# RWKV chunk loop: one run of products without the inverse ahead of the levels, the rest in pieces between them

## The reference, cut to what matters

```python
def _rwkv7_step(state, inputs):
    r, decay, kk, a, k, v = inputs
    sa = jnp.einsum("bhvk,bhk->bhv", state, kk)
    state = (state * decay[:, :, None, :]
             - sa[..., None] * (kk * a)[:, :, None, :]
             + v[..., None] * k[:, :, None, :])
    y = jnp.einsum("bhvk,bhk->bhv", state, r)
    return state, y
```

## Time and profile before

| what | us |
|---|---|
| runs of the kernel before: median (lowest to highest of 3) | 4284.13 (4281.7 to 4284.21) |
| the profiled execution, span from the first to the last instruction (the one time shown for it) | 4290.0 |
| TensorE busy in it | 4142.7 |
| chunk loop in it, first score products to first matmul of the tail | 3017.1 to 3757.2 |

### The profile page before, as it was taken

One profiled execution on the slowest core, in us unless ns is written; L12 is line 12 of the kernel. 1 busy time (PEld: TensorE's weight loads), 2 busy tenths in 40 slices (PEclk: granted clock), 3 DMA queues, 4 the chain that ended last, 5 costly groups with the idle time before them and its releaser, 6 DMA issues. The chain is left out here.

```text
span 4290.0 us, 90861 instructions
## 1 busy us (share of the span) xinstructions
PE 4142.7 (97%) x35784; PEld 3330.7 (78%) x35784; DVE 2381.1 (56%) x3103; ACT 1664.3 (39%) x3296; POOL 816.2 (19%) x657
## 2 busy tenths in 40 slices
PE   7999999997999999999999999999899999999999
PEld 7888899886788888887666666666788888888887
DVE  5344454443444444444888877777566667633222
ACT  4222222223222222222666666666344444421112
POOL 3101111112111111101000000000356666600222
PEclk9999999998999999999999999999999999999999
DMA  2333333334333333335434443443333333365553
GB/s 90 116 120 120 111 110 106 106 100 144 97 106 114 100 107 114 116 117 153 87 82 88 89 92 85 86 85 71 96 98 101 101 101 101 86 204 174 189 184 125
DMA packets 482569, 479.81 MB, mean 112 GB/s; under 512 B 256784, under 2 KB 366992, under 8 KB 476128
## 3 DMA queue, kind: packets, MB, share of 16 engines
q1 hardware_dynamic: 469360, 445.85, 37.3%
q10 hardware_dynamic: 11520, 25.17, 1.6%
q0 software_dynamic: 1392, 4.54, 0.4%
HBM read 305.51 MB, written 169.93 MB: 111 GB/s over the span
## 5 line engine op out<-in xcount | busy, mean ns | idle before, releaser
L1271 DVE TENSOR_TENSOR_SCAN kept<-keep,kept 128x512 f32<-128x512 f32 (+1 forms) x448 | 436.6, 974 | 60.2 <-ACT keep L1233 18.7
L1233 ACT ACTIVATE keep<-z 128x512 f32<-128x512 f32 (+3 forms) x704 | 342.7, 505 | 230.5 <-PE z L1166 218.7
L1176 PE MATMUL turned<-t_identity,kept 128*128 128x128 f32 (+1 forms) x2432 | 376.0, 276 | 22.5 <-DVE kept L1271 22.5
L1243 ACT COPY w<-turned 128x512 f32<-128x512 f32 (+4 forms) x704 | 363.1, 528 | 79.7 <-PE turned L1176 78.2
L1176 PEld LDWEIGHTS turned<-t_identity,kept 128*128 128x128 f32 (+1 forms) x2432 | 277.7, 135 | 134.1 <-ACT w L1243 45.6
L1268 DVE TENSOR_TENSOR_SCAN kept<-keep,hidden 128x512 f32<-128x512 f32 (+3 forms) x256 | 284.2, 1116 | 133.7 <-ACT keep L1233 133.1
L1203 PE MATMUL acc<-w,dv 128*64 128x512 f32 (+3 forms) x1280 | 317.1, 554 | 0.0
L1165 PE MATMUL z<-k_high,q_parts 128*128 128x512 f32 (+3 forms) x704 | 300.0, 427 | 8.5 <-PEq L2210 5.3
L1165 PEld LDWEIGHTS z<-k_high,q_parts 128*128 128x128 f32 x704 | 133.4, 189 | 158.6 <-ACT keep L1233 96.8
L1166 PE MATMUL z<-k_low,q_parts 128*128 128x512 f32 (+3 forms) x704 | 250.6, 360 | 0.0
L1742 POOL TENSOR_TENSOR off<-NT,tri 128x512 f32<-128x512 f32 x165 | 206.0, 1275 | 167.6 <-ACT NT L1646 167.6
(11 more groups left out here) (566 smaller groups left out, 10814.7 us busy)
## 6 DMA issues: line engine op xcount, KB each, us to landing
w_raw0A<-in_w_main SPq DMA_DIRECT2D x42, 512.0 KB, 3.9
w_raw0B<-in_w_main SPq DMA_DIRECT2D x42, 512.0 KB, 4.0
w_raw1A<-in_w_main SPq DMA_DIRECT2D x41, 512.0 KB, 4.0
w_raw1B<-in_w_main SPq DMA_DIRECT2D x41, 512.0 KB, 3.8
KB<-scr_kb SPq DMA_DIRECT2D x33, 512.0 KB, 5.2
AR<-scr_ar SPq DMA_DIRECT2D x33, 512.0 KB, 5.2
y_raw<-scr_y SPq DMA_DIRECT2D x64, 256.0 KB, 4.5
merge<-scr_merge SPq DMA_DIRECT2D x64, 256.0 KB, 5.3
```

What stands on the lines that cost most here:

```text
L1176: mm = pe.transpose(turned[num % TB][0:size, P * r:P * r + P], kept[kept_in(g)][:, src:src + size], t["identity"][:, :])
L1233: act.activation(keep[num % KB][:, 0:size], z[num % ZB][:, 0:size], ACT.Sigmoid, scale=-DH ** -0.5).then_inc(keep_done, 1)
L1243: act.copy(w[num % WB][0:size, c0:512], turned[num % TB][0:size, c0:512]).then_inc(copied, 1)
L1271: dve.tensor_tensor_scan(dst, data, data, kept[kept_in(g)][:, end:end + 1], ALU.mult, ALU.bypass).then_inc(scanned, 1)
```

## The change

In turn `n`, TensorE now runs in one piece: the next state of chunk n-2, the score products of n, the variance of n-3, all value products of n-2, the key transposes of n itself, and half of the right sides of n-1. Then come the levels, with these pieces after the product and after the advance:

| level | after the product | after the advance |
|---|---|---|
| 1 | right sides of n-1, pairs 4 to 6 | pair 7 |
| 2 | own values; state outputs of n-1, pairs 0 to 2 | own values; pair 3 |
| 3 | own values; updates of n-1, pairs 0 to 2 | own values; pair 3 |
| 4 | updates, pairs 4 to 6 | pair 7 |
| 5 | state outputs, pairs 4 to 6 | pair 7 |

The next state of a chunk thus moves a turn later. `S_sum` and the state multiply are now first on their engines in a turn, `R` stands in level 2, `LV` in level 3, the `VU` copies in level 4. On ScalarE root, square, copy of `y_bank`, turned keys and `sq_high` come right behind the `NT` copies. The first half of the reciprocals is taken in four columns of 128x64, one in level 3, one in level 4, two in level 5; the other half stays 128x256 at the start of the next turn. `sq_low` stands behind the `off` masks. The diff, cut to its core (`heads` yields the pairs and heads that were two loops before):

```diff
@@ sync @@
                 if inside(n, -1):
-                    reach(sp, "st_pe", n - 1)
+                    reach(sp, "kbt_pe", n - 1)
                     load_keys(n + 1, nb)
...
                     if n == 2:
-                        reach(sp, "s_pe", n - 1)
+                        reach(sp, "r_pe", n - 1)
                     load_queries(n + 1, nb)
@@ tensor @@
+            def next_state(m):
+                b = m % 3
+                reach(pe, "u_even", m + 1)
+                reach(pe, "u_odd", m + 1)
...
+            def variance(m, n):
+                reach(pe, "sq_high", m)
+                reach(pe, "sq_low", m)
+                reach(pe, "kbt_out", 2 * min(n, NCH) - 1)
...
             def turn_keys(n):
                 b = n % 3
-                pe.wait_ge(kb_in[b], 16 * (n // 3) + 16)
                 reach(pe, "lv_out", n)
-                reach(pe, "std_done", n - 4)
+                reach(pe, "std_done", n - 3)
...
+            def right_sides(m, ks):
+                b = m % 3
+                reach(pe, "s_done", m)
...
+            def updates(m, ks):
+                b = m % 3
+                reach(pe, "r_out", m + 1)
+                reach(pe, "t_out", 10 * m + 10)
...
+            def state_outputs(m, ks):
+                b = m % 3
+                reach(pe, "yc_out", m - 1)
...
                 def beside_product(lv):
-                    if lv <= 2 and inside(n, 0):
-                        own_values(2 * lv - 2)
-                    if 3 <= lv <= 4 and inside(n, 2, 1):
-                        value_part(lv - 1)
-                    if lv == LAST and inside(n, -1):
-                        turn_keys(n + 1)
+                    if lv in (2, 3) and inside(n, 0):
+                        own_values(2 * lv - 4)
+                    if lv == 1 and inside(n, 1):
+                        right_sides(n - 1, (4, 5, 6))
+                    if lv == 2 and inside(n, 1, 1):
+                        state_outputs(n - 1, (0, 1, 2))
+                    if lv == 3 and inside(n, 1):
+                        updates(n - 1, (0, 1, 2))
+                    if lv == 4 and inside(n, 1):
+                        updates(n - 1, (4, 5, 6))
+                    if lv == 5 and inside(n, 1, 1):
+                        state_outputs(n - 1, (4, 5, 6))
...
-                if inside(n, 3, 1):
-                    variance()
-                if inside(n, 2, 1):
-                    value_part(0)
-                    value_part(1)
-                if inside(n, 1) and n < NCH:
-                    next_state()
+                if inside(n, 2) and n <= NCH:
+                    next_state(n - 2)
+                if inside(n, 0):
+                    score_products(n, turn)
+                if inside(n, 3, 1):
+                    variance(n - 3, n)
+                if inside(n, 2, 1):
+                    value_products(n - 2)
+                if inside(n, 0):
+                    turn_keys(n)
+                if inside(n, 1):
+                    right_sides(n - 1, (0, 1, 2, 3))
                 for lv in range(1, LAST + 1):
...
-            turn_keys(0)
             walk(pe, body)
@@ vector @@
-                if inside(n, 1):
-                    reach(dve, "r_pe", n)
-                    reach(dve, "lv_out", n)
-                    dve.tensor_tensor(R[:, :, :], chain[:, :, :], LV[:, :, :], ALU.add).then_inc(s["r_out"], 1)
+                if inside(n, 2) and n <= NCH:
+                    reach(dve, "s_pe", n - 1)
+                    reach(dve, "s_done", n - 2)
+                    dve.tensor_tensor(S_sum[:, :, :], chain[:, :, :], S[b2][:, :, :], ALU.add).then_inc(s["s_sum"], 1)
                 if inside(n, 4, 1):
-                    inverse_std(n - 4, 1)
+                    inverse_std(n - 4, slice(HP, PAIRS))
...
+                    if lv in (3, 4) and inside(n, 3, 1):
+                        inverse_std(n - 3, slice(lv - 3, lv - 2))
+                    if lv == LAST and inside(n, 3, 1):
+                        inverse_std(n - 3, slice(2, 3))
+                        inverse_std(n - 3, slice(3, 4))
...
-                if inside(n, 3, 1):
-                    inverse_std(n - 3, 0)
@@ gpsimd @@
-                if inside(n, 3, 1):
-                    reach(pool, "sq_high", n - 3)
-                    tt(sq_low[:, :, :], yc_sq[:, :, :], sq_high[:, :, :].bitcast(F32), ALU.subtract, "sq_low")
+                if inside(n, 2) and n <= NCH:
+                    reach(pool, "s_sum", n - 1)
+                    reach(pool, "ys_pe", n - 4)
+                    tt(S[(b + 2) % 3][:, :, :], S_sum[:, :, :], t["w_end"][:, bass.ds(n - 2, 1), :].rearrange(
+                        "p o k -> p (o k)").unsqueeze(2).broadcast_to(grid), ALU.mult, "s_done")
```

More of the change, by code:

```diff
@@ L1548, in own_values @@
+            def state_outputs(m, ks):
+                b = m % 3
+                reach(pe, "yc_out", m - 1)
+                for k, h, hs in heads(ks):
+                    mm = pe.matmul(y_bank[hs, k, :], S[b][hs, k, :], AR[b][hs, k, 1, :], start=k == 0, stop=False,
+                                   skip_group_check=True)
+                if ks[-1] == PAIRS - 1:
+                    mm.then_inc(s["ys_pe"], 1)
+            def body(n, b, turn):
                 def own_values(quarter):
@@ L1551, in own_values @@
                     reach(pe, "st_out", 2 * n + 2)
[L1552 to L1555, removed]
+                    for k, h, hs in heads(range(2 * quarter, 2 * quarter + 2)):
+                        us = slice(DH * (1 - h), DH * (1 - h) + DH)
+                        mm = pe.matmul(lv_bank[hs, k, :], scores[h][b][us, k, 0:C], VU[b][us, k, h, :], start=True, stop=True)
                     if quarter == 3:
                         mm.then_inc(s["lv_pe"], 1)
-                def variance():
-                    reach(pe, "sq_high", n - 3)
-                    reach(pe, "sq_low", n - 3)
-                    if inside(n, 0):
-                        reach(pe, "kbt_out", 2 * n + 1)
-                    pe.matmul(var_bank[:, :, :], t["ones_sum"][:, :], sq_high[:, :, :], start=True, stop=False)
-                    pe.matmul(var_bank[:, :, :], t["ones_sum"][:, :], sq_low[:, :, :], start=False, stop=True).then_inc(s["var_pe"], 1)
                 def product(lv, half):
@@ L1573, in product @@
                         reach(pe, "t_out", 10 * n + 2 * (lv - 2) + half + 1)
[L1574 to L1578 removed]
+                    for k, h, hs in heads(range(HP)):
+                        mm = pe.matmul(x_bank(half)[hs, k, :], off[lv - 1][hs, HP * half + k, :], T2[hs, half, 0, k, :],
+                                       start=True, stop=True)
                     mm.then_inc(s["x_pe"], 1)
@@ new lines, in beside_advance @@
+                def beside_advance(lv):
+                    if lv in (2, 3) and inside(n, 0):
+                        own_values(2 * lv - 3)
+                    if lv == 1 and inside(n, 1):
+                        right_sides(n - 1, (7,))
+                    if lv == 2 and inside(n, 1, 1):
+                        state_outputs(n - 1, (3,))
+                    if lv == 3 and inside(n, 1):
+                        updates(n - 1, (3,))
+                    if lv == 4 and inside(n, 1):
+                        updates(n - 1, (7,))
+                    if lv == 5 and inside(n, 1, 1):
+                        state_outputs(n - 1, (7,))
@@ L1680, in body @@
                     act.copy(tail["y_hi"][n - 1][:, :], tail["y_raw"][n - 1][:, :]).then_inc(y_first_high, 1)
-            turned_keys(0)
             walk(act, body)
```

165 lines of the change are left out of this document (67 added, 98 removed).

## The result

The changed kernel takes 4257.1 us (median of 4 runs, 4255.6 to 4260.2) against 4282.9 for the kernel before beside it (4278.4 to 4284.2): ratio 0.9941, 95% interval 0.9929 to 0.9953. It is faster, by 25.8 us where 46 were forecast. The time lies in the range (4218 to 4268), 19 us above the number given and 1 us above the stretch called "my case" (4222 to 4256).

The account below looks back on a forecast made before the run. TensorE was taken to bound the kernel, paying for latency gaps in the levels and 1.96 us outside them. Savings of 31 (28 turns), 9 (turns 2 to 4), 2 (turns 0 and 1) and 4 (end): 4284 - 46 = 4238 us, range 4218 to 4268.

Parts of the forecast that it names:

- my case: Whole kernel: the prediction's own account, summed to 4238 us, stretch 4222 to 4256, chance 0.65.
- What bounds the kernel: Loop on TensorE: it pays for latency gaps in the levels, then 1.96 us of state outputs and right sides outside them.
- A turn without stalls: Loop turn: 5.6 ahead of the levels, 1.1 next state, 13.3 levels; 20.0 us against 21.08, so -1.1.
- The stretch ahead of the levels: Scores to first product: latency chain and TensorE's own work both give about 5.6 us, against 5.72: -0.1.
- The price of the pieces: Levels, at 30 ns a record: 1 and 4 at 2.57, 2 and 3 at 2.87, 5 at 2.40; sum 13.3 us.
- rival D: Levels: pieces run without restarts (12.9 us), stalls fall to 0.4; 1.8 us a turn gained, 4219 us; chance 0.08.
- The stalls: TensorE in the loop, read as late instructions: change between -0.4 and +0.6 us a turn, taken as 0.
- Rival C: Levels: TensorE starves for instructions, 3.5 us of stalls a turn against 0.72; slower, 4326 us; chance 0.05.
- The end: Last level to the tail's first matmul: chain of 18.3 us becomes 14, saving 4 us.
- The early turns: Turns 2 to 4: `R` leaves its place, 21.3 us each, -3.0 each, 9 in all; turns 0 and 1: 2 us.
- The other engines: VectorE, ScalarE, GpSimd, SP: moved work fits or is hidden, reciprocals by columns included; ScalarE has 0.7 us left.
- rival E: Level 1: ScalarE's spare 0.7 us is missing through late key transposes; 0.5 a turn back, 4252 us; inside the own case.

Follow-up runs that it names:

- The runs without loads: Keys, queries, values and gates not loaded from chunk 3 on, in either kernel: kernel before 4275.3 us (0.9976), changed kernel 4243.7 us (0.9904).
- the runs with more and fewer waits: TensorE waits, 20 more or 12 fewer a turn: kernel before 4316.1 or 4273.8 us, changed kernel 4286.7 or 4229.6 us.
- the first profile of before: The kernel before, unchanged, in the profile the prediction was made from: 4290.0 us, mean turn 21.80 us.
- the kernel with the fewest waits: The changed kernel with 17 waits a turn on TensorE instead of 34: 4219.3 us, ratio 0.9856 to the kernel before.
- the kernel before with fewer waits: The kernel before without 12 already passed TensorE waits a turn (21 instead of 33): 4273.8 us, ratio 0.9974 to the kernel before.
- the second profile: The kernel before, unchanged, profiled again: 4287.4 us (1 run), span 4285.6 us, mean turn 21.70 us.

## Why the prediction was right and where it was off

**What bounds the kernel: right.** The latency of a level is its floor: 2.46 by the sum, 2.48 in the changed kernel. The gaps in it could take the products that had stood outside, and 1.96 us of them are gone from between the last level and the scores. A turn without stalls was forecast at 20.0 and measured at 19.25.

**The stretch ahead of the levels: right.** First product at 5.6 by the sum, 5.66 measured; key transposes at 4.05, measured 4.15; the wait for the root 0.4, measured 0.34. The next state takes 1.08 and covers the last copy.

**The price of the pieces: too high.** The step that put levels 2 and 3 at "2.87 each" gave each of the moved records its 30 ns next to the own values. They took 2.52. In level 2 the 52 records up to the advance took 1.30 (3489.30 - 3488.00), 25 ns each, where the sum had 1.57; the own values run among the others there. Levels 1 and 4 were put at 2.57 and took 2.48 and 2.52; level 5 was put at 2.40 and took 2.48 without its pause. Together the levels take 12.5 where the sum had 13.3, and a turn without stalls was put 0.75 too long, 20 us over the loop. That is shorter than the levels of rival D (12.9), whose fewer stalls did not come.

**The stalls: the step that failed.** "it lies between -0.4 (hidden) and +0.6 a turn; I take 0, since the number of blocks stays." The number did stay (121 transfers in 27 turns in both kernels), but the stalls, taken as there (mean turn less a turn without any), went from 0.72 to 1.67 a turn (20.92 - 19.25). That is +0.95, over the upper end: 26 us over the loop, of which the cheaper pieces gave back 20. That the time still fell in the range is in part luck, two errors of opposite sign. The runs without loads show that what was added isn't traffic, the runs with more and fewer waits that it follows the number of waits in the stream. Rival C had the place and, by the reading of the instruction queue, the mechanism, and the wrong size: it needed 2.5 a turn to turn the sign, and 1.67 came. The sentence from the Trainium skill (Runtime: NRT & Kernel Launch, Instruction fetch mechanics), that the issue floor hides fetching, doesn't fit these traces: all 51 gaps of the changed kernel end 2.1 to 3.6 us after the start of an instruction transfer, and the old order gained 11 us by 12 instructions fewer of 1141, without a change in its shortest turn.

**The end: failed.** "I count 14" against 18.3, and 1.1 for turn 32. Nothing came. The end of the changed kernel, in the timeline of TensorE:

```profile
3707.72 0.62 PE L1490 MATMUL chain<-VU,KBt 128*64 128x64 f32 x14 [1.29 <-issue]
...
3714.72 1.15 PE L1518 MATMUL y_bank<-scores,VU 128*64 128x64 f32 x32 [0.25 <-ACT VU L1691]
3720.14 0.77 PE L1510 MATMUL flip<-sq_high,t_ones_sum 128*128 128x512 f32 x1 [4.27 <-issue]
3720.70 0.63 PE L1511 MATMUL flip<-sq_low,t_ones_sum 128*128 128x512 f32 x1
3722.41 0.77 PE L2072 MATMUL bb<-y_hi,tail_first_hi 128*128 128x512 f32 x1 [1.08 <-ACT rstd L1665]
```

I had counted 1.1 for turn 32 and 4 for the chain behind its last level. In the changed kernel that chain takes 3722.41 - 3705.64 = 16.8 against 18.3 in the first profile of before (17.8 in the second), and one pause of 1.29 us is in it. Turn 32 up to there takes 19.9 against 18.8 (18.2): the old turn 32 had no key transposes in its level 5 any more, so it had less to save than I counted, and the new one has pauses of its own (0.9 in one row of L1575). In the new order the next state of chunk 31 stands behind the last level, where in the earlier trace rows it was already done. From the last value products to the last variance it takes 5.4 (3714.72 to 3720.14) where it took 4.7 in the first profile of before. With few pauses on both sides the end does save something: 33.6 us in the kernel with the fewest waits against 35.3 in the kernel before with fewer waits.

**The early turns: right in size, half right in cause.** 3.0 each were forecast for turns 2 to 4, and against the second profile 2.4 each came (3.3 against the first); turns 0 and 1 gave 2.7 for 2. The three waits for `R` (4.7 us) are gone, as said. In their place TensorE waits 2.0 for transposes, 1.6 for the root and 0.9 for the state; the sum had 0.6 a turn for the last alone. The clock in turns 2 to 4 is 0.97 in the changed kernel, 0.93 and 0.98 in the two profiles of before, so against the second profile it is no part of this gain.

**The base.** The sum used a profile of 4290.0 with turns of 21.80; the second has 4285.6 and 21.70. That is 3 us of the miss in the 27 turns, 3 more in turns 2 to 4. From profile to profile the sum now closes: 46 forecast, less 26 for the stalls, 6 for the end and 6 for the base, plus 20 for the pieces and 2 for turns 0 to 4, is 30, and 30.0 was measured. The runs show 25.8; the runs of the kernel before had medians between 4281.3 and 4286.6 beside the different experiments, which is wide enough for the rest.

**The other engines: right.** The columns of the reciprocals changed nothing, as said, and rival E's late copies on ScalarE did not come: level 1 did not lengthen.

## What to carry to other kernels

Work put into the latency gaps of a chain of small products was nearly free here (0.07 us for 16 records, 0.47 outside), but the stream it makes is denser, and TensorE then has more pauses (1.67 us a turn, 0.72 before), which by the trace are waits for instructions. So count the wait instructions as well as the time, and look at the mean turn and at a turn without pauses apart; check that the shortest turn is one. Waits on semaphores that an engine has passed, or that another wait implies, are instructions too; leaving out 17 of 34 a turn gave more than the whole reordering (some 35 us and 26 us). And when work moves from one turn to the next, count the end of the loop from the same chunk, not from the same line.

## What the runs showed that I had not expected

A wait instruction on TensorE, long reached, costs 39 to 58 ns of the mean turn, though matmul and weight load together take 29. For the twelve left out this cost is wholly in pauses, in both kernels; for the twenty put in, 17 and 30 ns of it are not. The issue rows of the kernel before are 0.26 and 0.40 us a turn in its two profiles, 0.04 with 12 fewer waits, and 0.02 when the loop's loads were left out instead. And where own values stand among other products, the records follow each other at 25 ns, closer than the 29 of one kind.
